# First two modulation sections loaded and made by halves, the first halves ahead of the second, with buffers of their own for the gate's first factor

## What is computed

```python
m_l = (jax.nn.silu(c) @ w_mod[i] + b_mod[i])[:, None, :]
m_c = (jax.nn.silu(c_ctx) @ w_mod[i] + b_mod[i])[None, None, :]
sh1, sc1, g1, sh2, sc2, g2 = jnp.split(m_l, 6, axis=-1)
a_l = rmsnorm(x, norm_mix_g[i]) * (1.0 + sc1) + sh1
z = h @ w_in                     # q, k, v, g of four heads
z = (h @ gw1[d]) @ gw2[d] + gb[d]  # log gate, rank 16, d = 0, 1
```

## Time and profile before

| what | us |
|---|---|
| runs shown | 1710.3, 1713.78, 1712.42 (median 1712.42) |
| profiled execution, device time | 1713.71 |
| its span in the profile | 1711.8 |
| PE busy, share of the span | 1625.4, 95% |
| ACT, DVE, POOL busy | 523.1, 590.4, 596.5 |
| mean granted clock of TensorE | 0.98 |

### The profile page before, as it was taken

The page is one execution under the profiler, slowest core; times in us unless marked ns, Lnnn a source line. Parts: engine busy times, 40 slices in busy tenths (PEclk is TensorE's granted clock), DMA queues, the critical chain, the costliest instruction groups (busy, mean ns, idle before and its releaser), DMA issues. The chain is left out here.

```text
span 1711.8 us, 22709 instructions
## 1 busy us (share of the span) xinstructions
PE 1625.4 (95%) x10028; PEld 1358.6 (79%) x10028; DVE 590.4 (34%) x707; ACT 523.1 (31%) x574; POOL 596.5 (35%) x433
## 2 busy tenths in 40 slices
PE   6999999998899999999999997999977899999997
PEld 3788787877688888888888886888855688888885
DVE  3543333353331121111211124779984311111112
ACT  4434243322321211112111123477772322222222
POOL 2122211212222332323323244244474354454442
PEclk9899999999999999999999999999998999999999
DMA  9324234222233432334323322022212133232322
GB/s 319 103 81 121 80 94 124 75 75 79 70 99 99 124 98 75 99 99 122 100 75 99 93 84 90 31 74 74 74 50 74 61 95 96 92 99 98 99 80 80
DMA packets 199317, 160.64 MB, mean 94 GB/s; under 512 B 7234, under 2 KB 193972, under 8 KB 199220
## 3 DMA queue, kind: packets, MB, share of 16 engines
q1 hardware_dynamic: 198832, 159.08, 30.1%
q10 hardware_dynamic: 388, 0.12, 0.0%
HBM read 157.08 MB, written 2.10 MB: 93 GB/s over the span
## 5 line engine op out<-in xcount | busy, mean ns | idle before, releaser
L489 POOL TENSOR_TENSOR w_lo<-raw,w_hi 128x512 fp32r<-128x512 f32 (+1 forms) x404 | 576.2, 1458 | 1088.4 <-ACT w_hi L959 1088.4
L538 PE MATMUL duo<-a_hi,w_hi 128*128 128x512 f32 x1648 | 491.6, 358 | 47.8 <-DVE a_lo L1394 22.6
L541 PE MATMUL duo<-a_lo,w_hi 128*128 128x512 f32 x1648 | 485.9, 355 | 0.0
L544 PE MATMUL duo<-a_hi,w_lo 128*128 128x512 f32 x1648 | 485.7, 355 | 0.0
L959 ACT ACTIVATE w_hi<-raw 128x2048 fp32r<-128x2048 f32 (+1 forms) x101 | 192.3, 1905 | 549.1 <-PE duo L544 549.0
L538 PEld LDWEIGHTS duo<-a_hi,w_hi 128*128 128x128 f32 x1648 | 270.1, 190 | 107.0 <-issue 55.7
L544 PEld LDWEIGHTS duo<-a_hi,w_lo 128*128 128x128 f32 x1648 | 270.0, 190 | 45.5
L541 PEld LDWEIGHTS duo<-a_lo,w_hi 128*128 128x128 f32 x1648 | 270.0, 190 | 45.1
L1592 DVE TENSOR_TENSOR hid<-duo,gate 128x1024 f32<-128x1024 f32 (+1 forms) x33 | 33.5, 1043 | 524.0 <-PE duo L544 524.0
L538 PE MATMUL duo<-h_hi,w_hi 128*128 128x512 f32 (+1 forms) x528 | 160.5, 358 | 0.0
L544 PE MATMUL duo<-h_hi,w_lo 128*128 128x512 f32 (+1 forms) x528 | 159.6, 356 | 0.0
(11 more groups left out here) (229 smaller groups left out, 1457.6 us busy)
## 6 DMA issues: line engine op xcount, KB each, us to landing
raw<-in_ffn_w_dram SPq DMA_DIRECT2D x120, 512.0 KB, 4.9
mod_ring<-in_w_mod_dram SPq DMA_DIRECT2D x80, 512.0 KB, 5.3
raw<-in_gla_w_in_dram SPq DMA_DIRECT2D x24, 512.0 KB, 4.6
raw<-in_lru_w_in_dram SPq DMA_DIRECT2D x16, 512.0 KB, 4.2
raw<-in_ffn_w_dram SPq DMA_DIRECT2D x16, 384.0 KB, 3.8
mod_first<-in_w_mod_dram SPq DMA_DIRECT2D x4, 1024.0 KB, 14.5
mod_second<-in_w_mod_dram SPq DMA_DIRECT2D x4, 1024.0 KB, 14.2
raw<-in_gla_w_out_dram SPq DMA_DIRECT2D x8, 512.0 KB, 4.9
```

The lines of the kernel that those rows point to most:

```text
L489: pool.tensor_tensor(w_lo[b][:, k:k + 2, 0:cols], raw[b][:, k:k + 2, 0:cols], w_hi[b][:, k:k + 2, 0:cols].bitcast(F32), ALU.subtract).then ...
L538: pe.matmul(tile_out(ps, t, part, n), wh, act_hi[:, k, s:s + n], start=opens, stop=False, skip_group_check=True)
L541: pe.matmul(tile_out(ps, t, part, n), wh, act_lo[:, k, s:s + n], start=False, stop=False, skip_group_check=True)
L544: mm = pe.matmul(tile_out(ps, t, part, n), wl, act_hi[:, k, s:s + n], start=False, stop=last, skip_group_check=True)
```

## The change

The start's section weights lie in four buffers `mod_start[0..3]` of 512 columns each: first half of section 1, first half of section 0, second half of section 1, second half of section 0. 0 and 1 are loaded ahead of gate1 and qk, 2 and 3 behind them. PE makes the products of 0 and 1 and turns 0 before the norm sums, turns 1 after them; the products and turns of 2 and 3 go between the first three rows of the projection. The gain (1 + scale) is made by halves too (`start_gain`), and so the second halves are asked for only by row 4 (DVE) and by ACT's row 4. The eight products of one half all lie on alternating strips of one bank. The gate's first factor gets `gate1_hi` and `gate1_lo`, so v of head 0 is rounded right after the operand rows, without a wait for the rank-16 product. The context part of that product, which writes `vec_psum`, begins at k = 4. The first two pieces of section 2 are loaded without a wait for the start's products.

Places and loads (`gate1_lo` takes the space between `mod_start[2]` and `mod_start[3]`):

```diff
-        mod_first = place("mod_first", [P, 8, D], F32, H_AT)
-        mod_second = [place("mod_second0", [P, 8, 512], F32, A_AT), place("mod_second1", [P, 8, 512], F32, H_AT + 32 * KB)]
+        mod_start = [place(f"mod_start{i}", [P, 8, 512], F32, offset)
+                     for i, offset in enumerate((A_AT, A_AT + 16 * KB, H_AT, H_AT + 24 * KB))]
+        gate1_hi = place("gate1_hi", [P, 8, P], F32R, H_AT + 40 * KB)
+        gate1_lo = place("gate1_lo", [P, 8, P], F32R, H_AT + 16 * KB)
...
@@ -342,7 +343,8 @@
             def mod_pieces(s, *pieces):
                 v = w_mod[s // 6].rearrange("(k p) n -> p k n", p=P)
                 for p in pieces:
-                    sp.wait_ge(mod_used, 8 * (s - SEC_HEAD) + p + 1)
+                    if (s, p) not in ((SEC_HEAD, 0), (SEC_HEAD, 1)):
+                        sp.wait_ge(mod_used, 8 * (s - SEC_HEAD) + p + 1)
                     sp.dma_start(mod_ring[p % 2][:], v[:, :, bass.ds((s % 6) * D + p * P, P)]).then_inc(
                         mod_loaded[p % 2], 16)
 
...
-
-            def second_half(n):
-                c0 = SEC_FIRST[1] * D + n * 512
+
+            def start_piece(i):
+
+                c0 = SEC_FIRST[i % 2] * D + i // 2 * 512
                 for k in range(0, KT, 4):
-                    sp.dma_start(mod_second[n][:, k:k + 4], w_first[:, k:k + 4, c0:c0 + 512]
-                                 ).then_inc(second_loaded[n][k // 4], 16)
-
-            second_half(0)
+                    sp.dma_start(mod_start[i][:, k:k + 4], w_first[:, k:k + 4, c0:c0 + 512]
+                                 ).then_inc(start_loaded[i][k // 4], 16)
+
+            start_piece(0)
+            start_piece(1)
             sp.wait_ge(pads_made, 1)
             g1 = gla_gate_w1[0].rearrange("d (k p) r -> d p k r", p=P)
             load("gate1", (raw[0][:, :, 0:RANK], g1[0]), (raw[0][:, :, 32:32 + RANK], g1[1]))
@@ -386,7 +387,8 @@
...
             gate2_load(0)
             v_load(0)
@@ -482,14 +484,17 @@
             pool.wait_ge(pads_made, 3)
             pool.tensor_copy(mask[CHUNK:P, :, 0:CHUNK], mask[CHUNK:P, :, CHUNK:P]).then_inc(consts_made, 1)
...
-                    pool.tensor_tensor(w_lo[b][:, k:k + 2, 0:cols], raw[b][:, k:k + 2, 0:cols],
-                                       w_hi[b][:, k:k + 2, 0:cols].bitcast(F32), ALU.subtract).then_inc(lo_ready, 1)
-
-            low(0, P)
+                    pool.tensor_tensor(w_lo[b][:, k:k + 2], raw[b][:, k:k + 2], w_hi[b][:, k:k + 2].bitcast(F32),
+                                       ALU.subtract).then_inc(lo_ready, 1)
+
+            pool.wait_ge(hi_ready, 1)
+            for k in range(0, 8, 2):
+                pool.tensor_tensor(gate1_lo[:, k:k + 2], raw[0][:, k:k + 2, 0:P], gate1_hi[:, k:k + 2].bitcast(F32),
+                                   ALU.subtract).then_inc(lo_ready, 1)
```

PE:

```diff
+            def start_products(i):
+
+                if i >= 2:
+                    pe.wait_ge(half_ready, i - 1)
+                for k in range(KT):
+                    if k % 4 == 0:
+                        pe.wait_ge(start_loaded[i][k // 4], 16)
+                    g = 32 * (k % 4)
+                    mm = pe.matmul((mod_psum, vec_psum)[i % 2][g:g + 32, :], cs[:, k], mod_start[i][:, k], start=k < 4,
+                                   stop=k >= 4, tile_position=(0, g), skip_group_check=True)
+                mm.then_inc(start_used if i < 2 else mod_used, 1)
+
...
+            def start_turn(i):
+                pe.wait_ge(mod_rowed, i + 1)
+                if i == 0:
+                    pe.wait_ge(pick_made, 1)
+                for p in range(4):
+                    at_ = 512 * (i % 2) + p * P
+                    mm = pe.matmul((mod_psum, vec_psum)[i % 2][:, 2 * p:2 * p + 2], first_rows[:, at_:at_ + P], pick[:],
                                    start=True, stop=True, skip_group_check=True)
                 mm.then_inc(mod_turned, 1)
...
-            for k in range(KT):
-                if k % 2 == 0:
-                    pe.wait_ge(first_loaded[k // 2], 16)
-                g = 32 * (k % 4)
-                for n, ps in enumerate((mod_psum, vec_psum)):
-                    mm = pe.matmul(ps[g:g + 32, :], cs[:, k], mod_first[:, k, n * 512:(n + 1) * 512], start=k < 4,
-                                   stop=k >= 4, tile_position=(0, g), skip_group_check=True)
-            mm.then_inc(mod_used, 1)
-            first_turn(0, 0)
-            first_turn(0, 1)
+            start_products(0)
+            start_products(1)
+            start_turn(0)
             norm_sums(0, BOTH)
-            pe.wait_ge(mod_ready, 1)
-            second_products(0)
-            first_turn(1, 0)
-            second_products(1)
-            first_turn(1, 1)
+            start_turn(1)
...
-            hi, lo = w_hi[CH["gate1"] % 2], w_lo[CH["gate1"] % 2]
+            hi, lo = gate1_hi, gate1_lo
...
             for k in range(KT):
                 a_wait(("prep", 0, 0))(k)
                 low_rank(k, 0)
-                for j in ((), (), (0, 1, 2), (3,), (4,), (5,), (6,), (7,))[k]:
+                if k == 4:
+                    pe.wait_ge(mod_ready, 2)
+                for j in ((), (), (), (), (0, 1, 2, 3, 4), (5,), (6,), (7,))[k]:
                     mm = low_rank(j, 1)
                 if k == KT - 1:
                     done(mm)
                 for t in range(2):
                     mm = tile_row(("qk", 0), ("qk", 0), BOTH, a_hi, a_lo, 8, k, t, begin=t == 0)
+                if k == 0:
+                    start_products(2)
+                elif k == 1:
+                    start_turn(2)
+                    start_products(3)
+                elif k == 2:
+                    start_turn(3)
```

ACT and DVE (`start_section(i)` adds the bias to four feature rows, `start_gain(h)` makes four of the gain's):

```diff
@@ -992,14 +1001,14 @@
                     act.activation(ps, ps, ACT.Exp, scale=-0.5).then_inc(rooted, 1)
                 sec = 6 * layer + 3 * which
                 if n == 0:
-                    first_copy(1, 0)
                     high("gate1", None, P)
                     high(("qk", 0))
-                    act.wait_ge(half_ready, 1)
+                    act.wait_ge(half_ready, 2)
                 for m in range(KT):
-                    if n == 0 and m == 1:
-                        first_copy(1, 1)
+                    if n == 0 and m == 2:
+                        start_copy(2)
                     if n == 0 and m == 4:
+                        start_copy(3)
                         act.wait_ge(mod_ready, 2)
...
@@ -1054,11 +1063,13 @@
             for n in range(4):
                 if n == 2:
                     x_copy(3)
+                elif n == 3:
+                    start_copy(0)
                 wait_moved(act, ("turn", n))
                 square(0, n, TOK)
-            first_copy(0, 0)
-            first_copy(0, 1)
+            start_copy(1)
             prep(0, 0, BOTH)
+            high(("v", 0))
...
@@ -1067,7 +1078,6 @@
             wait_done(act, "tlow")
             steps.mark(act.activation(t_low[:, 0:LAT], duo("tlow")[0:64, 1, :], ACT.Copy))
             moved(act.activation(t_low[:, LAT:TOK], vec_psum[0:64, 0:CTX], ACT.Copy), "tlow")
-            high(("v", 0), "tlow")
...
@@ -1372,8 +1386,11 @@
 
                 scale(0)
                 for m in range(KT):
-                    if n == 0 and m == 2:
-                        second_section(1)
+                    if n == 0 and m == 3:
+                        start_section(2)
+                        start_gain(1)
+                    elif n == 0 and m == 4:
+                        start_section(3)
                         dve.wait_ge(mod_ready, 2)
                     if m + 1 < KT:
                         if m >= 1:
@@ -1417,10 +1434,9 @@
             steps.link(dve.tensor_tensor(pick[:], pick[:], ident[:, 64:66], ALU.add))
             dve.tensor_tensor(pick[:], pick[:], ident[:, 96:98], ALU.add).then_inc(pick_made, 1)
             x_copy(2)
+            dve.memset(gate2[:], 0.0).then_inc(gate2_zeroed, 1)
             for n in range(4):
                 add_squares(0, n, TOK)
-            section(0, SEC_FIRST[0])
-            dve.memset(gate2[:], 0.0).then_inc(gate2_zeroed, 1)
             prep(0, 0, BOTH)
```

More of the change, by code:

```diff
@@ L266, in build @@
         vec_loaded, x_loaded = sem("vec_loaded"), [sem(f"x_loaded{b}") for b in range(2)]
-        first_loaded = [sem(f"first_loaded{k}") for k in range(4)]
-        second_loaded = [[sem(f"second_loaded{n}_{k}") for k in range(2)] for n in range(2)]
-        second_used, half_ready = sem("second_used"), sem("half_ready")
+        start_loaded = [[sem(f"start_loaded{i}_{k}") for k in range(2)] for i in range(4)]
+        start_used, half_ready = sem("start_used"), sem("half_ready")
         vec_turned, vec_ready, cs_ready = sem("vec_turned"), sem("vec_ready"), sem("cs_ready")
@@ L388, in _ @@
             qk_load(0)
-            second_half(1)
+            start_piece(2)
+            start_piece(3)
             sp.wait_ge(gate2_zeroed, 1)
@@ L483, in _, with low @@
```

(19 more changed lines are left out.)

58 lines of the change are left out of this document (16 added, 42 removed).

## The result

The changed kernel takes 1718.99 us (median of 7 runs, 1717.14 to 1721.27) against 1712.42 (7 runs of before beside them): ratio 1.0037, 95% interval 1.0024 to 1.0050. It is slower by 6.6 us, and lies 0.4 us above the range that was given (1711.2 to 1718.6). The profiled execution took 1719.09 us with a span of 1717.1. The forecast of "no change that can be told" was wrong. Of the rivals, A (slower, by the clock) has the cause and comes nearest in time, though not by the sum that it gave.

The account below looks back on a forecast made before the run. PE, busy 1625.4 of 1711.8 us, was taken as the bound. Earlier start -3.0, moved work +5.2 and the stretch behind v +0.6 gave +2.8 us: 1715.2 against the median 1712.42, range 1711.2 to 1718.6.

Parts of the forecast that it names:

- no change that can be told: Whole kernel: 1715.2 us against the median 1712.42, inside the 3.4 us (0.2%) a measurement can tell; forecast's chance 0.52.
- A: Whole kernel, rival: slower because half clock follows PE's gaps and thin work; +6.1 us, 1718.5; chance 0.20.
- What bounds the kernel: First 102 us: PE's work bounds, with POOL releasing the first row and a serial ACT and DVE chain k's transposition.
- the gain at v: From the gate product through v: PE done 4.4 us sooner, of which only 0.2 reaches k's transposition.
- The loads: Start's loads: new order costs nothing; last opening load again at about 22.54, later ones covered by more than 10 us.
- Norm sums start at 24.5: -2.5 us: Opening on PE: last four products cost 0.96, half turn 0.9, so norm sums start at 24.5 in place of 26.98.
- Norm sums themselves: PE's norm sums before the first row: length kept at 5.8 us, with ends -1.2 and +2.2 for the range.
- The copy: ACT, ahead of the high parts: one copy of section rows (34.77 to 35.24) goes away, -0.5 us.
- the stretch from high part to first row: From ACT's high part to PE's first row, 35.24 to 45.09: left at 9.85 us, first row at 42.1.
- Moved work +5.2: Between PE's first rows: two sets of eight products and two turns, 2 x (1.7 + 0.9) us, ends 4.4 and 5.9.
- Behind v: From v to the first g row: -0.2 at k's transposition, together +0.6 us, ends -0.8 and +1.0.
- The two signs by which I would have been wrong: First head: gate product at or before 72 us, or PE not waiting before k's transposition.

Follow-up runs that it names:

- e2: The kernel before with only the gate's first factor in its own buffers and v rounded early; 1711.52 us, 0.9994 of before.
- e1: The changed kernel with the second halves' products and the first of their turns moved ahead of the wait for the first row; 1712.65 us, 0.9995 of before.
- e3: The changed kernel with 11 unread matmuls in PE's gap ahead of the first row; 1716.01 us, 1.0016 of before.
- e4: The changed kernel with four unread matmuls among the opening products, where PE waits for loads; 1714.87 us, 1.0015 of before.
- e5: e1 with e4's four unread matmuls and seven more between the pieces in PE's gap before the first row; 1710.27 us, 0.9982 of before.
- e6: e5 with three more unread matmuls ahead of k's transposition in the first head; 1708.69 us, 0.9972 of before.
- e8: e2 with unread matmuls: one during ScalarE's first section copy, six between the second section's pieces, three ahead of k's transposition; 1708.75 us, 0.9975 of before.

## Why the prediction was wrong, step by step

**What bounds the kernel** was read rightly. The marks and what releases them are those of the prediction: POOL the first row, PE's own work the gate product, the serial chain k's transposition. Gate product to transposition was to be as long as before but for 0.2; it is 25.59 in place of 25.73. e2 shows that this chain absorbs the gain at v. That gain was smaller than said: PE was ready for the transposition 22.6 us behind the gate product (103.80 less the wait of 3.01), 3.2 us sooner than before and not 4.4, because of the new wait of 1.17 for ScalarE's copy.

**The loads** were to cost nothing. The last of the opening came 0.63 us later (23.17 for 22.54), in a similar way in each of the kernels with halves (23.2 to 23.7), so it is no chance. The later loads were covered, as said.

**"Norm sums start at 24.5: -2.5 us" is the step that failed.** They started at 26.76: -0.2. Of the missing 2.3 us, 0.6 is the load. The last four products took 1.86 us (23.17 to 25.03) in place of 0.96, and the half turn 1.73 (25.03 to 26.76) in place of 0.9, both exactly at half clock: together 1.7. I had taken the price of products and turn from rows at full clock, and asked what a thinner opening does to the clock for the norm sums alone. But the change takes away more than half of what PE has to do while it waits for the loads (1.07 us of 4 from 19 to 23, before 2.70), and the clock fell ahead of these products. It did so in e1 too (0.72 from 19 to 23, 0.50 from 23 to 27, norm sums at 27.09), and in e3 it fell behind them, in the turn (0.74 from 23 to 27). e4, e5 and e6 fill this stretch and keep 1.00; e4 has the products at 1.0, the turn at 0.99 and the norm sums at 25.56.

**Norm sums themselves:** I kept 5.8; they took 5.7 (26.76 to 32.46). At full clock they take 4.1 in e4; the 4.6 that I had for it holds a wait of 0.18 and is from another place. **The copy** that is gone and the stretch from high part to first row: I had -0.5 and 9.85 left as it was; from the end of the norm sums (32.46) to the first row are 11.8 us, where before it was 12.3. Right. POOL was not blocked by VectorE in a new way: its two blocks took 2.79 and 5.56, together what the one of 8.35 took before, and a_lo again paid, with 3.20 us for the pair beside POOL. The Trainium skill's rule (SBUF — State Buffer, section Who interferes with whom) leaves it to the order of issue which of the two is blocked, so here the measurement decides.

**"Moved work +5.2":** 2.23 (49.63 to 51.86), 2.73 (54.75 to 57.48) and 0.81 (60.37 to 61.18) are 5.8, near the upper end, the first set partly at half clock. The first row at half clock to its end, +1.0, was not in the forecast's sum; rival A named it, as +0.8, but its sum leaves it out. This is the second term that was too small. Together, the gate product is -0.85 + 5.8 + 1.0, about +6 (measured +6.2), where I had +2.2.

**Behind v:** -0.1 at the transposition, then 4.3 us to the first g row in place of 3.8: +0.35 in all, where I had +0.6. Right. So the first g row is 6.5 us late where the forecast had 2.8: 2.1 of the missing 3.7 are the later first row (44.24 for 42.1), 1.8 the rows behind it, and -0.25 this last term.

**The choice between the cases.** Rival A had the right mechanism, and the point that decides it was named: a first row later than about 43. I gave it 0.20. That its price was nearly right (+6.1, 1718.5; measured +6.6, 1718.99) is in part luck. Its sum had +2.2 from norm sums at half clock to their end, and they took 5.7 us as in the forecast; it had +1.0 behind v, where +0.35 came. In their place stood the load (0.6), products and turn ahead of the norm sums at half clock (1.7), and the first row (1.0). The two signs by which I would have been wrong, a gate product at or before 72 and no wait ahead of k's transposition, look to the fast side only, and neither came.

The Trainium skill (TensorE: Matmul & The Clock Gate, section HAM oscillation) speaks of idle waits that put the work behind them at half rate. The trace agrees for the two long waits: 0.50 behind the one of 11.00 us, 0.68 behind the one of 3.01. The 0.52 in the opening stands behind two waits of 1.64 and 1.94 us with 1.07 us of work between them.

## What to carry to other kernels

Work that stood in front of a wait on the bounding engine cost next to nothing here; before such work is moved behind the wait, count it at full price (about 5 us here for two sets and a turn), and add what the emptied wait does to the clock of the work behind it (2.5 to 2.8 us for the first row, by e1 and e3). Before something is cut out of an engine's waiting time, look at what the granted clock does when the engine has less to do there: here a thinned opening was followed by half clock in the next products and the turn, and a gap of 11 us by half clock in a whole row, and matmuls that nobody reads bought back more (4.5 us below before in e6, 4.9 in e8) than the reordering alone (e1, no difference). And for a gain ahead of a mark, look at what else ends within half a microsecond of that mark: the chain from the gate product to k's transposition stayed at 25.6 us in eight of nine kernels, whatever was done to v.

## What was new about the hardware

The clock's fall is not the same in each execution of like code: e3 and the changed kernel have the same instructions up to 31 us, and the turn after the opening products took 1.28 us in one and 1.87 in the other, the last products 1.06 and 1.94. The kernel before and e2 have the same instructions on TensorE up to the end of the norm sums, which took 5.80 us in one (0.63 from 27 to 31) and 4.1 in the other (1.00). e4, e5 and e6, with the stretch filled, are alike: 1.05 and 1.07 in all three. So a single execution can carry 1 to 2 us of the clock's luck at a mark, in either kernel. The other thing is how much three matmuls of 128x512 can be worth: 1.2 to 2.5 us at the first g row of e6, for a wait of 3 us that was there anyway.
